# Between two branches of a two-layer decoder step, the inverse root and the scaled branch output are held in PSUM instead of SBUF

## The reference

```
def rms_norm(x, g):
    y = xf * lax.rsqrt(jnp.mean(xf * xf, axis=-1, keepdims=True) + NORM_EPS)
    return y * g
def ffn_half_step(x, g_pre, g_post, w_gate, w_up, w_down):
    return x + 0.5 * rms_norm(swiglu(rms_norm(x, g_pre), w_gate, w_up, w_down), g_post)
...
    for l in range(DEPTH):
        xp = ffn_half_step(xp, g[0], g[1], ffn1_gate[l], ffn1_up[l], ffn1_down[l])
        m_p, s_p = mix_prompt(rms_norm(xp, g[2]), lw)       # four mixers behind one projection w_in, then w_out
        xp = xp + rms_norm(m_p, g[3])
        xp = ffn_half_step(xp, g[4], g[5], ffn2_gate[l], ffn2_up[l], ffn2_down[l])
```

## Time and profile before

| | |
|---|---|
| median of 3 runs | 1516.01 us (1514.52 to 1517.2) |
| profiled execution | span of 1513.2 us from its first to its last instruction; no time beside the span is given for it |
| PE | busy 87% of the span |
| DVE | 60% |
| ACT | 41% |
| POOL | 15% |

### The profile page before, as it was taken

How to read it: one execution, slowest core, us unless ns; L and a number is a source line. 1 busy time by engine, 2 the same in 40 slices (tenths; PEclk the granted TensorE clock), 3 DMA queues, 4 the chain that set the end, 5 groups by cost and what they waited for, 6 DMA issues and landing times.

```text
span 1513.2 us, 27870 instructions
## 1 busy us (share of the span) xinstructions
PE 1314.4 (87%) x9864; PEld 1221.0 (81%) x9864; DVE 914.7 (60%) x1524; ACT 617.1 (41%) x1151; POOL 233.3 (15%) x238
## 2 busy tenths in 40 slices
PE   6999998995568779999989999799845888799997
PEld 5999988974456579999989999799623757699996
DVE  4676346567675557664476664654776565666544
ACT  4665354324120345443556644533420204544443
POOL 2000011006264020000110000200264521100000
PEclk9999998985578699999989999899765878999998
DMA  6565564553464235555646646544465424365553
GB/s 224 168 194 174 152 177 136 157 163 109 144 187 130 87 111 173 188 161 154 192 139 189 186 148 166 176 146 133 125 190 153 145 84 139 106 188 179 159 164 94
DMA packets 286119, 234.15 MB, mean 155 GB/s; under 512 B 19898, under 2 KB 282018, under 8 KB 286056
## 3 DMA queue, kind: packets, MB, share of 16 engines
q1 hardware_dynamic: 286056, 233.37, 50.3%
HBM read 228.65 MB, written 5.37 MB: 155 GB/s over the span
## 4 chain that ended last, share of the span: by engine, by line
PE 70%; DVE 16%; issue 6%; ACT 3%; DMA 2%; POOL 2%; SPq 0%; DVEq 0%; POOLq 0%; ACTq 0%
PE ps L1503 19%; PE ps L1504 19%; PE ps L1505 19%; DVE wlo L956 3%; PE ps L1731 2%; PE ps L1839 2%; PE ps L1838 2%; DVE nlo L1003 2%; DVE s L1203 1%; POOL kslot L934 1%; ACT whi L597 1%; DVE yt L986 1%; PE ps L1621 1%; DMA raw<-in_w_in_dram 1%; PE ps L1822 1%
## 5 line engine op out<-in xcount | busy, mean ns | idle before, releaser
L1503 PE MATMUL ps<-nhi,whi 128*128 128x264 f32 x1936 | 562.3, 290 | 44.8 <-DVE nlo L1003 34.4
L956 DVE TENSOR_TENSOR wlo<-raw,whi 128x1024 fp32r<-128x1024 f32 (+2 forms) x376 | 394.7, 1091 | 277.5 <-ACT whi L597 277.1
L1504 PE MATMUL ps<-nlo,whi 128*128 128x264 f32 x1936 | 556.3, 287 | 0.0
L1505 PE MATMUL ps<-nhi,wlo 128*128 128x264 f32 x1936 | 555.7, 287 | 0.0
L1503 PEld LDWEIGHTS ps<-nhi,whi 128*128 128x128 f32 x1936 | 372.9, 193 | 52.1 <-DVE nlo L1003 27.6
L597 ACT ACTIVATE whi<-raw 128x1024 fp32r<-128x1024 f32 (+2 forms) x376 | 336.8, 945 | 173.7 <-PE ps L1505 112.7
L1504 PEld LDWEIGHTS ps<-nlo,whi 128*128 128x128 f32 x1936 | 373.2, 193 | 0.2
L1505 PEld LDWEIGHTS ps<-nhi,wlo 128*128 128x128 f32 x1936 | 370.9, 192 | 0.0
L1503 PE MATMUL ps<-hhi,whi 128*128 128x264 f32 x704 | 204.1, 290 | 9.3 <-DVE hlo L973 9.1
L1505 PE MATMUL ps<-hhi,wlo 128*128 128x264 f32 x704 | 202.8, 288 | 0.0
L1504 PE MATMUL ps<-hlo,whi 128*128 128x264 f32 x704 | 202.4, 287 | 0.0
(11 more groups left out here) (343 smaller groups left out, 1432.5 us busy)
## 6 DMA issues: line engine op xcount, KB each, us to landing
raw<-in_ffn_gate_dram SPq DMA_DIRECT2D x44, 1024.0 KB, 5.3
raw<-in_ffn_up_dram SPq DMA_DIRECT2D x44, 1024.0 KB, 5.3
raw<-in_ffn_down_dram SPq DMA_DIRECT2D x64, 704.0 KB, 4.6
raw<-in_w_in_dram SPq DMA_DIRECT2D x24, 1024.0 KB, 5.7
kslot<-in_cache_fox_k_dram SPq DMA_DIRECT2D x128, 128.0 KB, 2.7
vslot<-in_cache_fox_v_dram SPq DMA_DIRECT2D x128, 128.0 KB, 2.5
raw<-in_w_out_dram SPq DMA_DIRECT2D x8, 1024.0 KB, 5.1
kslot<-in_state_swa_k_dram SPq DMA_DIRECT2D x32, 128.0 KB, 2.7
```

The costliest lines, as they stand in the source:

```text
L956: tt2(wlo[s][:, a:b], raw[s][:, a:b], whi[s][:, a:b].bitcast(F32), ALU.subtract).then_inc(S(f"w_lo{s}"), 1)
L1503: mm(out, wh, hi_, start=first, stop=False)
L1504: mm(out, wh, lo_, start=False, stop=False)
L1505: return mm(out, wl, hi_, start=False, stop=last)
```

## The change

The inverse root of odd norms is written to bank 6 of PSUM instead of `r_post`, which no longer exists. The product of line 986 goes to bank 4 or 5 in turn instead of back to `yt`, and line 987 reads it there. At the end, the transposed output uses banks 0 to 3, one per tile, instead of two banks per tile, so that banks 4 to 6 are free. Number and order of the instructions on all engines are the same as before; only operands differ (and all SBUF addresses behind `r_post`, by 1056 bytes a partition). Lines 180 to 985 of the kernel before stand one line further up in the changed one (Ln and Exp in 633 and 634); from 986 on the numbers are the same.

```
-        r_post = place("r_post", [P, N])
...
-                        r = r_post[:, :] if e % 2 else r_pre
+                        r = ps[:, 6, 0:N] if e % 2 else r_pre
                         ch(act.activation(r, ps[:, 7, 0:N], ACT.Ln, bias=C("eps")))
                         act.activation(r, r, ACT.Exp, scale=-0.5).then_inc(S("rms"), 1)
...
-                    act.activation(xin[:, 0:2, t * P:(t + 1) * P], ps[:, 2 * (t % 4), 0:L].rearrange("p (a n) -> p a n", a=2), ACT.Copy).then_inc(S("y_taken"), 1)
-                    act.activation(xin[0:B, 2, t * P:(t + 1) * P], ps[0:B, 2 * (t % 4) + 1, 0:P], ACT.Copy).then_inc(S("y_taken"), 1)
+                    act.activation(xin[:, 0:2, t * P:(t + 1) * P], ps[:, t % 4, 0:L].rearrange("p (a n) -> p a n", a=2), ACT.Copy).then_inc(S("y_taken"), 1)
+                    act.activation(xin[0:B, 2, t * P:(t + 1) * P], ps[0:B, t % 4, L:L + P], ACT.Copy).then_inc(S("y_taken"), 1)
...
                         for t in range(KT):
-                            ch(stt(yt[:, t, :], yt[:, t, :], gain(l, e, t), r_post[:, :], ALU.mult, ALU.mult))
-                            tt2(x[:, t, :], x[:, t, :], yt[:, t, :], ALU.add).then_inc(S("x_new"), 1)
+                            u = ps[:, 4 + t % 2, 0:N]
+                            ch(stt(u, yt[:, t, :], gain(l, e, t), ps[:, 6, 0:N], ALU.mult, ALU.mult))
+                            tt2(x[:, t, :], x[:, t, :], u, ALU.add).then_inc(S("x_new"), 1)
...
-                        pe.transpose(ps[:, 2 * (t % 4), a * P:(a + 1) * P], x[:, t, a * P:(a + 1) * P], ident)
-                    pe.transpose(ps[0:B, 2 * (t % 4) + 1, 0:P], x[:, t, L:N], ident).then_inc(S("y_turned"), 1)
+                        pe.transpose(ps[:, t % 4, a * P:(a + 1) * P], x[:, t, a * P:(a + 1) * P], ident)
+                    pe.transpose(ps[0:B, t % 4, L:L + P], x[:, t, L:N], ident).then_inc(S("y_turned"), 1)
```

## The result

The changed kernel takes 1501.6 us (median of 4 runs, 1497.33 to 1507.26), the kernel before 1516.07 us (4 runs, 1514.52 to 1517.2): a ratio of 0.9908, with a 95% interval of 0.9883 to 0.9933, so 14.5 us less. Forecast were 8.4 us less, in a range that ended at 1504.5. The direction was right and the gain too small.

What follows compares the result with a forecast made beforehand. PE was taken to bound most of the time, with DVE costing where PE waits in five seams. Five times 1.68 us gave 8.4, with 0 for the writes: 1516.0 - 8.4 = 1507.6 us, range 1504.5 to 1512.7.

Steps and rivals of the forecast that it cites:

- The lock: In five seams: lines 986, 987 and POOL stop delaying each other; two tiles take 2.91 us, not 3.47; 1.68 a seam.
- The price of the write: Lines 986 and 987: cost of PSUM operands taken as 0, between +0.155 us and -0.034 us per instruction.
- the upper bound: Line 986's PSUM write doubles the fixed part, +0.155 us each, 5.1 us in all; as rival 1512.7 us, chance 0.13.
- The errata rule: Lines 986 and 987: 65 ns more for a PSUM operand, 4.3 us in all, leaving 4.1 us gain, not 8.4.
- The end of `by_tile`: In each seam, from the first line 986: 10.96 + 0.06 + 1.56 = 12.58 us, against 14.26 before.
- PE's floor: In the seam: PE, starting at 3.86 us and slow for 27 matmuls, finishes at 12.59 us, so can just follow.
- The root in PSUM: Closing norm: Exp reads PSUM, a gain of 0.03 us; in the five seams its price is hidden.
- Behind the seam: After `by_tile`, 24 matmuls, mean matmul, root and weight split are chained to it, so the 8.4 us carries through.

Runs made afterwards that it cites:

- POOL last: Kernel before, with POOL's even-norm additions waiting for all 8 squares instead of 2: 1511.77 us in one run, beside 1516.41 for the kernel before.
- the product alone: Changed kernel with the odd-norm root back in SBUF (`r_post`), only line 986's product in PSUM: 1497.54 us (5 runs), ratio 0.989.
- where DVE was made earlier still: Changed kernel with POOL's even-norm additions waiting for seven squares, plus three constant matmuls at each of four joints: 1496.94 us (4 runs), ratio 0.9873.
- the joints filled: Three constant matmuls added at each of four PE rests: kernel before 1510.21 and 1509.12 us, changed kernel 1499.55 and 1500.09 us.
- its repetition: The kernel before run again with no edit: 1515.27 us (11 runs, 1511.51 to 1517.28).
- the moved addresses: Kernel before with `r_post` placed last, so later SBUF addresses move by 1056 bytes: 1515.49 us (11 runs), ratio 1.0.
- the root alone: Changed kernel with line 986 writing back to `yt` in SBUF, only the odd-norm root in PSUM: 1511.1 us (6 runs), ratio 0.996.
- POOL late: Changed kernel with POOL's even-norm additions waiting for seven squares instead of two: 1501.79 us (6 runs), ratio 0.9905.

## Why the prediction was wrong, and where it was right

*The lock* held, to a few hundredths: 2.91 us for two tiles, 10.98 to 11.00 us to the low half of tile 6 (forecast 10.96). That POOL's additions are its cause is shown by the kernel with POOL last, and that the second SBUF input of line 987 is what matters most by the product alone. *The price of the write* was rightly put near 0: 8 ns with the product alone, 4 with the root in PSUM too, not the 155 of the upper bound. The errata rule of the Trainium skill ("VectorE: DVE Perf Modes"), worked out in the prediction as an estimated 65 ns for an operand from PSUM, which would have halved the gain, is not borne out here: line 987 takes 428 ns with one, against 433 for the same form from SBUF with no POOL addition beside it. *The end of `by_tile`* was forecast at 12.58 and is 12.74 to 12.79; the prediction reckons the last 12 matmuls 0.17 too short, for the kernel before as well (14.26 against 14.42 to 14.45), so the difference came out right. PE could follow, as forecast, and where DVE was made earlier still, PE's floor showed in two seams of five. *The root in PSUM* shortened Exp from 422 to 375 ns, by 0.047 us (0.03 forecast), with no trace in the end of the kernel: the closing stage is 12.02 and 12.03 us.

**The step that failed** is *Behind the seam*: "everything is chained to `by_tile` [...] So I carry the 8.4 us through to the end." The chain of semaphores does carry it: with the joints filled, the feed-forward stretches are the same within 0.5 us in both pairs, and beside the scatter of the mixers the seams alone differ. What the step took for granted is that PE does the same work in the same time behind the seam, in both kernels and in every execution. It does not. After the same rest PE was at 0.50 for 3.4 us in one execution and not in another, and each such stretch costs 1.5 us. Of the clock the prediction asked only in `by_tile`; no rival and no term of the range stood for it elsewhere.

In numbers, by medians over all runs: unfilled 1516.0 - 1503.7 = 12.3 us, filled 1509.4 (13 runs) - 1500.0 (8 runs) = 9.4 us. Of the 12.3, the seams are 8.3. The joints are put at 12.3 - 9.4 = 2.9. By the times alone this is not clear of noise: resampling the runs gives 9 to 16 us for the first figure, 8.6 to 11.9 for the second and -0.9 to 6.5 for their difference. What bears it out is the traces: the unfilled profiles with the whole of the old seam have 4, 3 and 2 stretches behind their joints, those of the changed kernel and of the product alone 1, 1 and 2, and the difference of 1.7 on average is 2.6 us at 1.5 each. The filling saves the kernel before 6.7 us and the changed kernel 3.7, in both cases some 2 us more than their stretches cost; that part is not traced. The last 1.1 lies in the stretches with the mixers or in the spread of the runs, and is not settled: the two stretches together take 598.0 to 603.8 us in the seven profiles with the product in SBUF and 595.9 to 601.1 in the seven with it in PSUM. The first comparison, 14.5, had the further luck of four runs whose median lay 2 us under that of all nine.

**What stays open** is why executions with the operands of before nearly always have the stretches. Behind the second to fourth joints, the three profiles of before, its repetition and the moved addresses have 8 of 9; the two of the changed kernel and that of the product alone 2 of 9. These are three executions a side, and the joints of one execution need not be independent, so the shares are rough. The seam's length as such does not sort them: the root alone, with nearly the old seam, has none of those three, POOL last has two, and the changed kernel with POOL late, with the shortest seam of the change, has two. Nor do the operands, which are the same in the changed kernel with and without POOL late; but one profile of each is too little to rule either out. The Trainium skill ("TensorE: Matmul & The Clock Gate", Part 1, What's actually happening) says that the number of slow matmuls at the start of one and the same kernel varies from run to run; the repeated profiles show such a variation behind the joints, but not what sets the shares. Whether another kernel that moves these joints by 1.7 us would win or lose by it can't be said from these runs.

## What to carry to other kernels

Where DVE runs beside POOL additions in SBUF, put one operand of each two-input DVE instruction into PSUM if a bank is free, and first the passing product whose reader has another input in SBUF. Where PE rests for some 2 us in the middle of a stage, try a few matmuls into a bank that is free at the time: here that was worth 6.7 us in the kernel before and 3.7 in the changed one, and it made the changed kernel's times steady enough to read a small change in them. A forecast that carries a gain through a long stretch of matmuls needs a term for the clock, also where the change touches nothing; here that was some 3 us in 12.

## What the runs showed of the hardware that was not expected

The same wait of 2.37 to 2.38 us, at the first joint of the same program, was followed by 3.4 us at a granted clock of 0.50 in one execution and by none in the next, for the kernel before as for the changed one. Filled down to 0.54 to 0.96 us it never was, at any of 20 joints in five profiles.

An instruction of DVE with two SBUF inputs (lines 987 and 1003, 264 elements) that begins under a POOL addition ends 0.29 us after POOL's end, whenever it began: in all profiles here the distance is 0.29 or 0.30. Line 1003 took 0.78 and 0.56 by it, line 987 0.86 or 0.71. Free of each other both pay nothing: POOL's first addition went from a mean of 834 ns to 751, line 987 from 568 to 428.

Three more matmuls at each of four joints, which nobody needs, made the kernel before 6.7 us faster, beside 9.4 us for the change itself where both kernels have them.
